# A transformer block on one core: the first layer norm, its modulation and the first projection in another order

## The chip, the core and the metric

The kernel runs on one NeuronCore of one Trainium2 chip. The core has a matrix engine (PE, TensorE), a vector engine (DVE), a scalar engine (ACT), a general engine (POOL) and a queue engine (SP) that here only issues DMA loads. Engines run side by side and wait for each other by semaphores. The metric is the device time of one execution in microseconds (us), and of several executions the median.

## The reference

The program computes two transformer blocks on 256 tokens of width 1024 in float32. Only its beginning is touched:

```python
mod = jax.nn.silu(c) @ cond_w + cond_b              # (1, 6144)
shift1, scale1, gate1, shift2, scale2, gate2 = jnp.split(mod, 6, axis=-1)
h = layer_norm(x) * (1.0 + scale1[:, None, :]) + shift1[:, None, :]
p = h @ w_in                                        # 1024 -> 2816
u = p[..., :512] * jax.nn.sigmoid(p[..., 512:1024])
# ... a causal convolution of u, a recurrence over the rest of p, an expert layer,
# and a second block with attention, a gated recurrence and a feed-forward layer
```

## The kernel before, in words

Weights stream through a ring of four slots of 2 MB. `weight_blocks` lists them in the order of their loads: a name, the slot, and the matmul job after which the slot is free. SP goes through this list in order, and where a slot was used before it waits until that job is computed, holding back every later load. `cond` blocks hold 512 columns of `cond_w`, `w_in` blocks 512 columns of `w_in`.

PSUM has eight banks. `JOBS` lists PE's work in order, each job with the engine (`act` or `dve`) that empties its bank. `assign_banks` gives banks to the jobs in rotation, and `begin` makes PE wait until the job that had the bank before was emptied. A job is a small group of matmuls: a shift of the rotation changes what a later job waits for.

The first stage goes as follows. DVE normalises the two tiles of 128 tokens into `xn`. For each of four blocks (order 2, 0, 3, 1; blocks 2 and 3 are `scale1`, 0 and 1 `shift1`) PE multiplies silu(c) with the block in four strips (`modp`, L809), DVE adds the bias into `mod_sum` (L2113), and PE adds the strips up with a matrix of ones, so that every partition holds the same 512 values (`mod`, L815). DVE multiplies and adds them onto 512 columns of `xn` (L2130, L2137). PE transposes those columns (`x_T`, L795), ACT copies them to `hT` (L1525). So the left 512 features (blocks 2 and 0) are ready before the right 512 (blocks 3 and 1).

Then comes the projection of 1024 features, eight groups of 128 (`k`). Jobs `in_conv` 2 and 3 make the gate half, 0 and 1 the other half, each 256 outputs for 256 tokens. `in_conv` 2 takes plain float32 matmuls (L782, two records each). All others are split: weight and input are each cut into a rounded high part and the rest, and three products high x high, high x low and low x high go into one sum (L840 to L842, 48 products for one job). The high parts are made by ACT (`hi_h1` L1583, `hi_in` L1590), the low ones by DVE (L2145, L2150). Between `in_conv` 2 and 3 PE transposes the parameter vectors (`params`, L872), which ACT copies to `col`. ACT takes the sigmoid of `in_conv` 2 and 3 (L1598), and its order is written out: four `hi_h1`, three `hi_in`, then the first sigmoid.

From there the work is one long chain over all engines; no part of it is touched, apart from banks that come in another rotation.

Of the kernel before, what the change touches and what calls it, by code (L numbers as in the profile page):

```python
# [77 lines left out]
IN_TWO_BANKS = ("inv_w", "inv_n")  # L78
# [94 lines left out]
BEGINS_AHEAD = {("query", 4): [("y2", 0, i) for i in range(2)], ("mem_T", 0, 0): [("y2", 1, i) for i in range(2)]}  # L173


HELD_FROM = {("in_rw", 6): (("conv_acc",), 1), ("query", 1, 0): (("h2_P", 0), 2), ("y2", 0, 0): (("h2_P", 1), 2)}
HELD_UNTIL = {("conv_mean",): (("conv_acc",), 1), ("mem_T", 0, 0): (("h2_P", 0), 2), ("mix_T", 0, 0): (("h2_P", 1), 2)}


def assign_banks():  # L180
    bank_of, before = {}, {}
    job_in, kept, turn = [None] * BANKS, set(), 0
    for job, _ in JOBS:
# [12 lines left out]
        if job in bank_of:  # L196
            kept.remove(bank_of[job])
            continue
        ahead = BEGINS_AHEAD.get(job, [])
        for j in ahead + [job]:  # L200
            n = 2 if j[0] in IN_TWO_BANKS else 1
# [6 lines left out]
            if j in ahead:  # L208
                kept.add(b)
# [51 lines left out]
def block_kernel(nc, A, out):  # L261
    ctx = ExitStack()
    with ctx:
# [13 lines left out]
        emptied = {"act": sem("emptied_by_act"), "dve": sem("emptied_by_dve"), "dots": sem("u_free"), "conv": sem("conv_ready")}  # L277
# [5 lines left out]
        turn["conv_acc",] = ("conv", 1)  # L283
        for t in range(NT):
            turn["h2_P", t] = ("dots", (t + 1) * PEER_H * TOPK)
        h2_banks = [PS[:, BANK_OF["h2_P", t]:BANK_OF["h2_P", t] + 2, :].rearrange("p a b -> p (a b)") for t in range(NT)]

        def bank(*name):
            return PS[:, BANK_OF[name], :]

# [105 lines left out]
        xn = at(12800, NT, D)  # L396
        chunk_decay = st[:, 32:48].rearrange("p (a b) -> p a b", b=NCH)
# [84 lines left out]
        def source(kind, *i):  # L482
# [5 lines left out]
            if kind == "cond":  # L488
                return lambda s: [(slot_cols(s, 512), cols(A["cond_w"], 512 * i[0], 512 * i[0] + 512))]
            if kind in ("w_in", "w_in_2"):  # L490
# [47 lines left out]
        for name, s, _ in BLOCKS:  # L538
            loads = source(*name)(s)
            landed[s] += 16 * len(loads)  # L540
# [21 lines left out]
        def loaded(eng, *name):  # L562
            s, n, _ = place[name]
            eng.wait_ge(slot_in[s], n)
# [24 lines left out]
        def _(sp):  # L589
# [3 lines left out]
            for name, s, free_after in BLOCKS:  # L593
                loads = place[name][2]
                if s in before and loads:
# [156 lines left out]
        def _(pe):  # L752
# [8 lines left out]
            def begin(*name):  # L761
# [4 lines left out]
                for job in JOB_BEFORE[name]:  # L766
                    was_emptied(pe, *job)
                return two_banks(*name) if name[0] in IN_TWO_BANKS else bank(*name)

# [2022 lines left out]
```

## Time and profile before

| | |
|---|---|
| median of three runs | 1421.1 us (1416.89, 1421.1, 1421.59) |
| the profiled execution's own time | 1416.83 us |
| its span, first to last instruction | 1414.4 us |
| mean granted TensorE clock | 0.904 of full |
| busy PE / DVE / ACT / POOL | 81% / 62% / 36% / 40% |
| chain that ended last | PE 51%, issue 12%, POOL 11%, DVE 11%, DMA 8%, ACT 3% |

Busy shares are averages over stages with other limits. The chain is read by its pieces: each has what was worked on, and the next one begins where the last one released it.

### The profile page before, as it was taken

To read this page: it belongs to the slowest core of one execution; us is meant where nothing else is said; L and a number is where in the kernel's file an instruction comes from. 1 tells how busy PE (TensorE), PEld (TensorE's weight loads), DVE (VectorE), ACT (ScalarE), POOL (GpSimd) and SP (SyncE) were. 2 spreads that over 40 slices of the span, in tenths; PEclk is the share of its full clock that TensorE was granted. 3 is DMA by queue.
4 is the path that set the end of the run, shared out by engine and by line. 5 is a ranking of instruction groups with operands and counts; after the bars stand their busy time and mean duration, and the time that the engine had idled before them with its cause. 6 is when DMAs were issued, how large, how long until landed. Compare 5 with 4: busy or idle time off the path is not lost.

```text
span 1414.4 us, 18085 instructions
## 1 busy us (share of the span) xinstructions
PE 1140.7 (81%) x6572; PEld 752.3 (53%) x6572; DVE 880.6 (62%) x1692; ACT 507.5 (36%) x1100; POOL 565.1 (40%) x641
## 2 busy tenths in 40 slices
PE   4999799848987757775879577767769998899997
PEld 1877564734553323332344233323329986799985
DVE  3588666854456458645685586567376575588763
ACT  1574332232241323222433233132216554366551
POOL 5064500325536666666756666766630000000000
PEclk9999999979999887887889888878789999899999
DMA  9372626588979999999999999999995425355440
GB/s 353 130 253 69 233 83 218 216 318 299 377 277 385 356 375 349 377 361 365 375 324 351 362 368 370 375 371 372 353 339 206 152 68 171 127 186 165 179 141 30
DMA packets 139775, 381.14 MB, mean 269 GB/s; under 512 B 10707, under 2 KB 37742, under 8 KB 139706
## 3 DMA queue, kind: packets, MB, share of 16 engines
q0 software_dynamic: 73728, 268.47, 50.3%
q1 hardware_dynamic: 64656, 108.87, 22.3%
q10 hardware_dynamic: 1322, 2.85, 0.6%
q8 instruction: 47, 0.77, 0.2%
q14 instruction: 22, 0.18, 0.0%
HBM read 379.10 MB, written 1.05 MB: 269 GB/s over the span
## 4 chain that ended last, share of the span: by engine, by line
PE 51%; issue 12%; POOL 11%; DVE 11%; DMA 8%; ACT 3%; another core or an unknown queue 1%; DVEq 1%; ACTq 0%; SPq 0%; POOLq 0%
PE banks L1222 12%; PE banks L840 7%; PE banks L842 7%; PE banks L841 7%; POOL arena L740 6%; POOL arena L733 5%; PE banks L1176 4%; DMA arena<-in_peer_u,arena 4%; DVE arena L2446 4%; DMA arena<-in_peer_v,arena 3%; PE banks L782 3%; DMA weight_ring<-in_cond_w 2%; PE banks L1157 1%; PE banks L809 1%
## 5 line engine op out<-in xcount | busy, mean ns | idle before, releaser
L1222 PE MATMUL banks<-arena 128*128 128x512 f32 x1008 | 494.4, 654 | 179.7 <-issue 120.5
L1222 PEld LDWEIGHTS banks<-arena 128*128 128x128 f32 x1008 | 210.3, 212 | 460.8 <-issue 402.1
L2446 DVE SCALAR_TENSOR_TENSOR arena<-arena,banks 128x1024 f32<-128x1024 f32 x256 | 306.9, 1220 | 202.6 <-DMA arena<-in_peer_u,arena 169.9
L740 POOL DMA_INDIRECT arena<-in_peer_v,arena x256 | 242.8, 948 | 199.7 <-PE banks L1222 104.6
L733 POOL DMA_INDIRECT arena<-in_peer_u,arena x256 | 243.9, 953 | 80.7 <-issue 73.8
L842 PE MATMUL banks<-hi_h,low_slot 128*128 128x256 f32 (+2 forms) x600 | 170.0, 283 | 0.0
L1785 ACT ACTIVATE arena<-arena 128x8 f32<-128x8 f32 x32 | 6.7, 208 | 350.9 <-issue 226.5
L842 PEld LDWEIGHTS banks<-hi_h,low_slot 128*128 128x128 f32 (+2 forms) x600 | 111.9, 187 | 0.2
L840 PE MATMUL banks<-hi_h,hi_w 128*128 128x256 f32 (+1 forms) x352 | 100.8, 286 | 1.5 <-DVE lo_h L2556 1.5
L841 PE MATMUL banks<-lo_h,hi_w 128*128 128x256 f32 (+1 forms) x352 | 99.4, 282 | 0.0
L1780 ACT ACTIVATE arena<-ident,arena 128x128 f32<-128x128 f32 x256 | 78.3, 388 | 4.9 <-issue 4.2
L1792 ACT ACTIVATE arena<-arena 128x128 f32<-128x128 f32 x252 | 77.1, 388 | 3.4 <-issue 0.5
L1176 PE MATMUL banks<-hT,weight_ring 128*128 128x128 f32 (+1 forms) x384 | 62.9, 323 | 14.9 <-issue 13.4
L698 POOL TENSOR_TENSOR arena<-arena 128x512 f32<-128x512 f32 x30 | 43.0, 1434 | 73.2 <-ACT arena L1640 71.7
L1176 PEld LDWEIGHTS banks<-hT,weight_ring 128*128 128x128 f32 x384 | 57.4, 203 | 21.2 <-issue 16.1
L840 PEld LDWEIGHTS banks<-hi_h,hi_w 128*128 128x128 f32 (+1 forms) x352 | 66.6, 189 | 1.7 <-DVE hT L2538 1.7
L841 PEld LDWEIGHTS banks<-lo_h,hi_w 128*128 128x128 f32 (+1 forms) x352 | 66.7, 189 | 0.0
L2737 DVE SCALAR_TENSOR_TENSOR arena<-banks,col,arena 128x255 f32<-128x255 f32 (+3 forms) x88 | 38.4, 477 | 30.2 <-ACT arena L2046 29.4
L2567 DVE TENSOR_TENSOR low_slot<-weight_ring,hi_w 128x2048 fp32r<-128x2048 f32 (+1 forms) x22 | 49.3, 2242 | 1.7
L721 POOL COPY arena<-arena 128x16 uint32<-128x16 uint32 x16 | 3.3, 204 | 103.0 <-DVE arena L2426 103.0
L2046 ACT ACTIVATE arena<-banks,col 128x256 f32<-128x256 f32 (+1 forms) x44 | 22.5, 562 | 56.2 <-PE banks L842 56.2
L1533 ACT ACTIVATE st<-st,eps 128x1 f32<-128x1 f32 x18 | 5.1, 293 | 102.3 <-DVE st L2098 52.0
(394 smaller groups left out, 1908.0 us busy)
## 6 DMA issues: line engine op xcount, KB each, us to landing
weight_ring<-in_cond_w SPq DMA_DIRECT2D x12, 2048.0 KB, 9.3
weight_ring<-in_w_in SPq DMA_DIRECT2D x11, 2048.0 KB, 8.0
weight_ring<-in_ffn_w_up SPq DMA_DIRECT2D x20, 1024.0 KB, 6.8
weight_ring<-in_ffn_w_down SPq DMA_DIRECT2D x5, 2048.0 KB, 7.7
weight_ring<-in_w_out SPq DMA_DIRECT2D x4, 2048.0 KB, 7.7
weight_ring<-in_peer_wq SPq DMA_DIRECT2D x4, 2048.0 KB, 8.0
arena<-in_peer_u,arena POOLq DMA_INDIRECT x256
arena<-in_peer_v,arena POOLq DMA_INDIRECT x256
```

The lines of the kernel that those rows point to most:

```text
L698: signal(g.tensor_tensor(conv[:, 2:4, :], conv[:, 2:4, :], taps(k), ALU.add), sem("taps_added"))
L733: g.indirect_dma_start(u_rows[:, j, :], None, A["peer_u"], bass.IndirectOffsetOnAxis(ap=row, axis=0)).then_inc(sem(f"u_in_{j}"), 16)
L740: g.indirect_dma_start(v_rows[:, j, :], None, A["peer_v"], bass.IndirectOffsetOnAxis(ap=row, axis=0)).then_inc(sem(f"v_in_{j}"), 16)
L840: mm(out_, sh, mh, start=first, stop=False)
L841: mm(out_, sh, ml, start=False, stop=False)
L842: return mm(out_, sl, mh, start=False, stop=last)
L1176: last = mm(b[:, half * n:half * n + n], w[:, k, f * P:f * P + P], hT[:, k, tok], start=(k == 0), stop=(k == KD - 1))
L1222: last = mm(acc[i], diag[:, r, j, :], v_rows[:, j, i * 512:(i + 1) * 512], start=False, stop=ends and j == 7)
L1780: fn(gate_diag[:, j, :], ident[:, :], ACT.Copy, scale=gates[:, bass.ds(n * TOPK + (8 * r + j), 1)])
L1792: ins = fn(diag[:, r, j, :], gate_diag[:, j, :], ACT.Copy, scale=gz[:, r, j:j + 1])
L2446: ins = v.scalar_tensor_tensor(out=u_rows[:, j, :], in0=u_rows[:, j, :], scalar=1.0, in1=h2_banks[t], op0=ALU.mult, op1=ALU.mult, accum_ou ...
L2567: signal(v.tensor_tensor(dst, w, hi_w[:, i % 4, :, 0:n], ALU.subtract), sem("up_split"))
```

## The change

Seven things are changed, all but the last in the stage up to `in_conv` 3:

1. PE transposes all of `xn` as soon as it is normalised, 16 transposes, into four banks that are held for it (`x_P`).
2. For blocks 0 to 3 the sum over strips is taken the other way round: `mod_sum` is the stationary operand and one column of ones the moving one, four matmuls of one column. The result is 4 columns with a feature on each partition. DVE copies them to `mod_col` and adds 1 to the scale.
3. ACT makes `hT` from the transposed banks with scale and shift as columns, one instruction for each of the eight groups. DVE's four multiplications and four additions over 512 columns go.
4. `w_in` block 1 (for `in_conv` 2 and 3) is loaded in two halves of 1 MB: groups 0 to 3 as third load, ahead of `cond` 3 and 1, with a semaphore of its own; groups 4 to 7 behind `cond` 1. `cond` 2 goes to slot 3, which `cond` 1 takes over, so SP waits for `modp` 2 there.
5. PE does groups 0 to 3 of `in_conv` 2 ahead of `modp` 3, and of `in_conv` 3 ahead of `mod` 3. The other halves stand where the whole jobs stood.
6. ACT and DVE make the high and low parts for both in halves too.
7. `in_conv` 2 and 3 take two banks each, and the rotation of banks changes for the jobs behind them, up to the expert layer.

```diff
-IN_TWO_BANKS = ("inv_w", "inv_n")
+IN_TWO_BANKS = ("inv_w", "inv_n", ("in_conv", 2), ("in_conv", 3))
@@ JOBS
-JOBS += part_jobs(3)
-JOBS += [(("x_T", t, 0), "act") for t in range(NT)]
-JOBS += modulation_jobs(3) + part_jobs(1) + modulation_jobs(1) + [(("x_T", t, 1), "act") for t in range(NT)]
+for _b in (3, 1):
+    JOBS += part_jobs(_b) + modulation_jobs(_b)
@@ banks
+BEGINS_AHEAD = {("modp", 3): [("in_conv", 2)], ("mod", 3): [("in_conv", 3)], ...
+HELD_FROM = {("modp", 2): (("x_P", 0), 2), ("mod", 2): (("x_P", 1), 2), ...
+HELD_UNTIL = {("modp", 3): (("x_P", 0), 2), ("in_conv", 0): (("x_P", 1), 2), ...
@@ weight_blocks
-    blocks = [(("cond", 2), 0, ("modp", 2)), (("cond", 0), 1, ("modp", 0)), (("cond", 3), 2, ("modp", 3)),
+    blocks = [(("cond", 2), 3, ("modp", 2)), (("cond", 0), 1, ("modp", 0)), (("w_in_ahead", 1), 0, None), (("cond", 3), 2, ("modp", 3)),
               (("cond", 1), 3, ("modp", 1)), (("w_in", 1), 0, ("in_conv", 3)), (("w_in", 0), 1, ("in_conv", 1)),
@@ PE
             def modulation(i):
...
+                if i < 4:
+                    for c in range(4):
+                        last = mm(b[:, c:c + 1], mod_sum[:, c * P:(c + 1) * P], ones[:, 0:1], start=True, stop=True)
+                    done(last)
...
+            def conv_tiles(half):
+                b, w = both_tiles("in_conv", 2), weights(512, "w_in", 1)
+                for e in range(2):
+                    for k in range(4 * half, 4 * half + 4):
+                        if e == 0:
+                            pe.wait_ge(sem("hT_ready"), k + 1)
+                        last = mm(b[:, e, :], w[:, k, e * P:(e + 1) * P], hT[:, k, :], start=(k == 0), stop=(k == KD - 1))
+                return last
...
+            for t in range(NT):
+                pe.wait_ge(sem("xn_ready"), t + 1)
+                for k in range(KD):
+                    last = nc.tensor.transpose(x_turned(k)[:, t * P:(t + 1) * P], xn[:, t, k * P:(k + 1) * P], ident[:, :])
+            last.then_inc(sem("x_turned"), 1)
...
+            early("in_conv", 2)
+            loaded(pe, "w_in_ahead", 1)
+            conv_tiles(0)
             mod_parts(3)
-            input_T(0)
+            early("in_conv", 3)
+            split_conv_tiles(0)
             modulation(3)
             mod_parts(1)
             modulation(1)
@@ ACT
+            def modulated(half):
+                act.wait_ge(sem("x_turned"), 1)
+                was_emptied(act, "mod", half)
+                for k in range(4 * half, 4 * half + 4):
+                    signal(fn(hT[:, k, :], x_turned(k), ACT.Identity, scale=mod_col[:, k:k + 1], bias=mod_col[:, 8 + k:9 + k]),
+                           sem("hT_ready"))
+                for k in (4 * half, 4 * half + 2):
+                    act.wait_ge(sem("hT_ready"), k + 2)
+                    signal(fn(hi_h1[:, k:k + 2, :], hT[:, k:k + 2, :], ACT.Copy), sem("h1_high"))
...
+            modulated(0)
             act.wait_ge(consts_ready, 1)
-            for p in range(3):
+            loaded(act, "w_in_ahead", 1)
+            signal(fn(hi_in[0][:, 0:4, :], in_columns(slot, *SPLIT_IN[0])[0][:, 0:4, :], ACT.Copy), sem("in_high"))
+            modulated(1)
+            in_high(0, slice(4, 8))
+            for p in range(1, 3):
                 in_high(p)
@@ DVE
+            def modulation_columns(i):
+                computed(dve, "mod", i)
+                at_ = 4 * (i % 2) + (0 if i >= 2 else 8)
+                empty(v.tensor_scalar(mod_col[:, at_:at_ + 4], bank("mod", i)[:, 0:4], 1.0, 1.0 if i >= 2 else 0.0, ALU.mult, ALU.add),
+                      "mod", i)
...
+            for half in range(2):
+                for i in (2 + half, half):
+                    mod_bias(i)
+                    modulation_columns(i)
+                low_h1(half)
+                in_low(0, slice(4 * half, 4 * half + 4))
+            for p in range(1, 3):
                 in_low(p)
```

How the rows move is shown at three places. The first is PE in the middle of the four modulation blocks, before: `slot_in_2` is the semaphore of the load of `cond` 3, `mem_kv` holds silu(c) and `mod_sum`.

```order
L809 MATMUL banks<-weight_ring,mem_kv 32x512 [waits slot_in_2]
L809 MATMUL banks<-weight_ring,mem_kv 32x512 x7
L795 MATMUL banks<-ident,arena 128x128 [waits h_ready,emptied_by_dve]
L795 MATMUL banks<-ident,arena 128x128 x7
L815 MATMUL banks<-mem_kv,ones 128x512 [waits emptied_by_dve,emptied_by_act]
L809 MATMUL banks<-weight_ring,mem_kv 32x512 [waits slot_in_3,emptied_by_dve]
L809 MATMUL banks<-weight_ring,mem_kv 32x512 x7
```

The same place now (L854 is the float32 projection, L834 `modp`, L871 to L873 the split products, of which 24 follow):

```order
L854 MATMUL banks<-hT,weight_ring 128x256 [waits ahead_in,hT_ready]
L854 MATMUL banks<-hT,weight_ring 128x256 [waits hT_ready] x3
L854 MATMUL banks<-hT,weight_ring 128x256 x4
L834 MATMUL banks<-weight_ring,mem_kv 32x512 [waits slot_in_2,emptied_by_dve]
L834 MATMUL banks<-weight_ring,mem_kv 32x512 x7
L871 MATMUL banks<-hi_h_54,hi_in_56 128x256 [waits h1_split,in_split,emptied_by_dve]
L872 MATMUL banks<-lo_h_55,hi_in_56 128x256
L873 MATMUL banks<-hi_h_54,low_slot_49 128x256
```

The transposes are gone from here, and half of `in_conv` 2 stands ahead of the strips of `cond` 3.

The second place is PE around the parameter transposes (128x54 is the first of them), before:

```order
L782 MATMUL banks<-hT,weight_ring 128x256 [waits slot_in_0,emptied_by_dve,emptied_by_act]
L782 MATMUL banks<-hT,weight_ring 128x256 x15
L872 MATMUL banks<-ident,arena 128x54 [waits emptied_by_act,params_in,consts_ready]
L872 MATMUL banks<-ident,arena 128x124
L872 MATMUL banks<-ident,arena 128x42
L872 MATMUL banks<-ident,arena 128x88 x2
L840 MATMUL banks<-hi_h_54,hi_in_56 128x256 [waits in_split,emptied_by_act,h1_split]
L841 MATMUL banks<-lo_h_55,hi_in_56 128x256
L842 MATMUL banks<-hi_h_54,low_slot_49 128x256
```

And now:

```order
L854 MATMUL banks<-hT,weight_ring 128x256 [waits slot_in_0,hT_ready]
L854 MATMUL banks<-hT,weight_ring 128x256 [waits hT_ready] x3
L854 MATMUL banks<-hT,weight_ring 128x256 x4
L926 MATMUL banks<-ident,arena 128x54 [waits emptied_by_act,params_in,consts_ready]
L926 MATMUL banks<-ident,arena 128x124
L926 MATMUL banks<-ident,arena 128x42
L926 MATMUL banks<-ident,arena 128x88 x2
L871 MATMUL banks<-hi_h_54,hi_in_56 128x256 [waits h1_split,in_split,emptied_by_dve]
L872 MATMUL banks<-lo_h_55,hi_in_56 128x256
```

Half the projection is left on either side. The bank of the parameter transposes was that of an `x_T` job before; now it is the first bank of `in_conv` 2, which ACT empties with its sigmoid.

The third place is ACT from `hT` to the first sigmoid, before. `hi_in` are the high parts of weights, `col` the parameters.

```order
L1525 ACTIVATE hT<-banks 128x4x128 [waits mm_done] x4
L1583 ACTIVATE hi_h_54<-hT 128x4x128 [waits emptied_by_act] x4
L1590 ACTIVATE hi_in_56<-weight_ring 128x2048 [waits slot_in_0,consts_ready]
L1590 ACTIVATE hi_in_57<-weight_ring 128x2048 [waits slot_in_1]
L1590 ACTIVATE hi_in_58<-weight_ring 128x2048 [waits slot_in_1]
L1598 ACT_TABLE_LOAD
L1598 ACTIVATE arena<-banks 128x2x256 [waits mm_done]
L1602 ACTIVATE col<-banks 128x396 [waits mm_done]
L1598 ACTIVATE arena<-banks 128x2x256 [waits mm_done]
```

And now:

```order
L1634 ACTIVATE hT<-banks,st 128x256 [waits emptied_by_dve,x_turned]
L1634 ACTIVATE hT<-banks,st 128x256 x3
L1638 ACTIVATE hi_h_54<-hT 128x512 [waits hT_ready] x2
L1650 ACTIVATE hi_in_56<-weight_ring 128x1024 [waits ahead_in,consts_ready]
L1634 ACTIVATE hT<-banks,st 128x256 [waits emptied_by_dve,x_turned]
L1634 ACTIVATE hT<-banks,st 128x256 x3
L1638 ACTIVATE hi_h_54<-hT 128x512 [waits hT_ready] x2
L1645 ACTIVATE hi_in_56<-weight_ring 128x1024 [waits slot_in_0]
L1645 ACTIVATE hi_in_57<-weight_ring 128x2048 [waits slot_in_1]
L1645 ACTIVATE hi_in_58<-weight_ring 128x2048 [waits slot_in_1]
L1658 ACT_TABLE_LOAD
L1658 ACTIVATE arena<-banks 128x2x256 [waits mm_done]
```

Three conversions and the table load still stand ahead of the first sigmoid; the first of them is a half, its other half being done before.

## Rows read from the trace of the kernel before

**Rows 1.** The chain that ended last, 0 to 120 us: start us, us, what.
```profile
2.83 22.32 DMA weight_ring<-in_cond_w
25.20 3.03 PE banks L809 x16
...
30.70 1.96 PE banks L809 x16
32.76 0.76 DVE mem_kv L2113
...
36.20 1.98 PE banks L795 x8
...
38.86 9.17 PE banks L782 x32
48.03 0.95 PE banks L872 x5
...
66.01 0.70 DVE arena L2164
66.78 1.92 ACT hi_in L1590
...
107.77 14.03 PE banks L782 x64
```
**Rows 2.** Timeline of PE, 0 to 49 us: start, us, operation, idle before.
```profile
11.60 3.64 PE L809 MATMUL banks<-weight_ring,mem_kv 128*32 128x512 f32 x16 [8.06 <-DMA weight_ring<-in_cond_w]
17.95 1.92 PE L809 MATMUL banks<-weight_ring,mem_kv 128*32 128x512 f32 x16 [0.62 <-DMA weight_ring<-in_cond_w]
20.83 1.12 PE L815 MATMUL banks<-mem_kv,ones 128*128 128x512 f32 x2 [0.95 <-DVE mem_kv L2113]
```
**Rows 3.** Timeline of ACT, 38 to 73 us.
```profile
38.70 2.18 ACT L1583 ACTIVATE hi_h<-hT 128x512 fp32r<-128x512 f32 x4
40.78 5.50 ACT L1590 ACTIVATE hi_in<-weight_ring 128x2048 fp32r<-128x2048 f32 x3
46.30 1.28 ACT L1598 ACT_TABLE_LOAD   x1
48.07 0.60 ACT L1598 ACTIVATE arena<-banks 128x512 f32<-128x512 f32 x1 [0.49 <-PE banks L782]
...
54.71 0.60 ACT L1598 ACTIVATE arena<-banks 128x512 f32<-128x512 f32 x1 [5.19 <-PE banks L842]
...
72.78 0.82 ACT L1609 ACTIVATE arena<-banks,keep_mu 128x256 f32<-128x256 f32 x2
```
**Rows 4.** Timeline of DVE, 34 to 50 us.
```profile
42.71 6.70 DVE L2150 TENSOR_TENSOR low_slot<-weight_ring,hi_in 128x2048 fp32r<-128x2048 f32 x3 [0.86 <-ACT hi_in L1590]
49.55 0.17 DVE L2155 TENSOR_SCALAR keep_ka<-col 128x4 f32<-128x4 f32 x1
```
**Rows 5.** Stretches of 2 us: five engines' busy us (count), PEclk, DMA share, GB/s.
```profile
26.00:28.00 2.00, 2.00 (x12) 0.21 (x4) 0.00 (x0) 0.00 (x0) 0.00 (x0) 0.50 1.06 389
...
40.00:42.00 2.00, 2.00 (x6) 1.54 (x5) 1.85 (x4) 2.00 (x3) 0.00 (x0) 0.50 1.08 360
```
**Rows 6.** Stretches of 2 us behind a pause of PE, later in the kernel.
```profile
172.00:174.00 2.00, 0.00 (x0) 0.00 (x0) 0.60 (x1) 0.00 (x0) 0.00 (x0) 1.00 0.95 354
...
176.00:178.00 2.00, 2.00 (x65) 2.00 (x63) 1.19 (x2) 0.00 (x0) 0.00 (x0) 0.51 0.03 8
178.00:180.00 2.00, 2.00 (x65) 1.88 (x61) 1.93 (x5) 1.19 (x2) 0.00 (x0) 0.63 0.00 0
```
**Rows 7.** Timeline of PE, 1208 to 1223 us: split products at either clock.
```profile
1218.05 0.41 PE L841 MATMUL banks<-lo_h,hi_w 128*128 128x256 f32 x1
...
1220.18 0.41 PE L842 MATMUL banks<-hi_h,low_slot 128*128 128x256 f32 x1
...
1220.95 0.28 PE L841 MATMUL banks<-lo_h,hi_w 128*128 128x256 f32 x1
...
1222.14 0.28 PE L842 MATMUL banks<-hi_h,low_slot 128*128 128x256 f32 x1
```

More of the change, by code:

```diff
@@ L196, in assign_banks @@
         if job in bank_of:
-            kept.remove(bank_of[job])
+            kept -= set(range(bank_of[job], bank_of[job] + banks_of(job)))
             continue
@@ L283, in block_kernel @@
         turn["conv_acc",] = ("conv", 1)
+        for i in range(2):
+            turn["x_P", i] = ("turned", 4 * i + 4)
         for t in range(NT):
@@ L539, in block_kernel @@
             loads = source(*name)(s)
+            if name[0] == "w_in_ahead":
+                place[name] = (s, 16, loads)
+                continue
             landed[s] += 16 * len(loads)
@@ L814, in modulation @@
                 was_emptied(pe, "modp", i)
-                done(mm(b, ones[:, :], mod_sum, start=True, stop=True))
-            def input_T(i):
-                was_emptied(pe, "mod", i)
-                pe.wait_ge(sem("h_ready"), i + 1)
-                for t in range(NT):
-                    b = begin("x_T", t, i)
-                    done(transposes(b, [xn[:, t, (4 * i + q) * P:(4 * i + q + 1) * P] for q in range(4)]))
+                if i < 4:
+                    for c in range(4):
+                        last = mm(b[:, c:c + 1], mod_sum[:, c * P:(c + 1) * P], ones[:, 0:1], start=True, stop=True)
+                    done(last)
+                else:
+                    done(mm(b, ones[:, :], mod_sum, start=True, stop=True))
@@ new lines, in conv_tiles, with split_conv_tiles @@
+            def conv_tiles(half):
[6 more added lines that the diff above has]
+                return last
+            def split_conv_tiles(half):
+                b = both_tiles("in_conv", 3)
+                pe.wait_ge(sem("h1_split"), 2 * half + 2)
+                pe.wait_ge(sem("in_split"), half + 1)
+                for e in range(2):
+                    f = slice(e * P, (e + 1) * P)
+                    for k in range(4 * half, 4 * half + 4):
+                        last = products(b[:, e, :], (hi_in[0][:, k, f], in_columns(low, "in_conv", 3)[0][:, k, f]),
+                                        (hi_h1[:, k, :], lo_h1[:, k, :]), k == 0, k == KD - 1)
+                return last
@@ new lines, in products @@
+            def products(out_, stationary, moving, first, last):
+                (sh, sl), (mh, ml) = stationary, moving
+                mm(out_, sh, mh, start=first, stop=False)
+                mm(out_, sh, ml, start=False, stop=False)
+                return mm(out_, sl, mh, start=False, stop=last)
+            assert not any(JOB_BEFORE["x_P", 0] + JOB_BEFORE["x_P", 1])
+            for t in range(NT):
+                pe.wait_ge(sem("xn_ready"), t + 1)
+                for k in range(KD):
+                    last = nc.tensor.transpose(x_turned(k)[:, t * P:(t + 1) * P], xn[:, t, k * P:(k + 1) * P], ident[:, :])
@@ L834, in _ @@
             modulation(1)
-            input_T(1)
-            was_emptied(pe, "x_T", 1, 1)
-            def products(out_, stationary, moving, first, last):
-                (sh, sl), (mh, ml) = stationary, moving
-                mm(out_, sh, mh, start=first, stop=False)
-                mm(out_, sh, ml, start=False, stop=False)
-                return mm(out_, sl, mh, start=False, stop=last)
             def split_in(kind, i):
@@ L1597, in _ @@
                 computed(act, "in_conv", i)
-                empty(fn(u_pad[:, 2 * (i - 2):2 * (i - 2) + 2, CONV_K - 1:], bank("in_conv", i).rearrange("p (a b) -> p a b", a=2),
-                         ACT.Sigmoid), "in_conv", i)
+                empty(fn(u_pad[:, 2 * (i - 2):2 * (i - 2) + 2, CONV_K - 1:], both_tiles("in_conv", i), ACT.Sigmoid), "in_conv", i)
                 if i == 2:
```

95 lines of the change are left out of this document (45 added, 50 removed).

## The prediction

> **What bounds the kernel now.** Read the chain that ended last first, in order of time [rows 1]. Up to 25.2 us it is the load of the modulation blocks; then come the strips of `cond` 3 and `cond` 1 on PE (L809), DVE's bias (L2113), the sum, the transposes, and at 38.86 `in_conv` 2 (L782) with 9.17 us and the parameter transposes with 0.95 us. From 49.0 to 66.0 PE works through three split jobs without a pause, and what follows is released by their ends: DVE at 66.01, ACT at 66.78. So a microsecond by which the first split job, `in_conv` 3, ends earlier is a microsecond off the whole, as long as PE then goes on. It ended at 54.6: ACT, which waited for it, starts its second sigmoid at 54.71 [rows 3]. That moment is what I forecast; the rest of the kernel is carried along.
>
> Next read ACT by its timeline [rows 3]. It is idle before 38.7 but for two copies, then it is full: four `hi_h1` (2.18), three `hi_in` (5.50), a table load (1.28), free at 47.6. There it waits 0.49 us for `in_conv` 2 and starts the first sigmoid at 48.07. Two engines arrive at nearly the same moment, and the change shortens PE's way only. Last read PE's granted clock in stretches of 2 us [rows 5]: 0.50 of full, that is 1.2 GHz, at 26 to 28 and at 40 to 42, each time behind pauses for loads or for DVE.
>
> **The first half, worked out.** `cond` 0 lands before 17.95 and its sum ends at 21.95 [rows 2]. The sum is now 8 passes with one column each, which the trace doesn't show. From above it is bounded by 8 transposes of 128 columns at the low clock, 1.98 us for L795 [rows 1], from below by half of the old sum, 0.5; I take the old 1.1. DVE's copy of 4 columns: 0.17, as L2155 [rows 4]. ACT's four `hT` of 128x256 from PSUM: 0.41 each, as L1609 (0.82 for two) [rows 3], so 1.64. PE has `hT` groups 0 to 3 at 24.0 (bounds 23.4 and 24.9). The half block of `w_in` has landed by then: it adds 1.05 MB behind `cond` 0, at some 389 GB/s [rows 5] 2.7 us, so about 20.7.
>
> `conv_tiles(0)` is 16 records. At full clock one takes 14.03/64 = 0.22 us [rows 1], so 3.5; at the low clock 2.00/6 = 0.33 [rows 5], so 5.3. It ends at 27.5 to 29.3. `cond` 3 landed at 25.2; with 1.05 MB more ahead of it that is 27.9, so it costs PE next to nothing. `modp` 3: 1.92 to 3.03 [rows 1, 2], I take the end at 31.0. Then 24 split products. At full clock one starts every 1.19/10 = 0.12 us, at the low clock every 2.13/10 = 0.21 [rows 7], so 2.8 or 5.1; I take 2.8, PE being busy since 24. With `mod` 3 PE is free at 34.9.
>
> **The second half.** `cond` 1 had landed by 30.70, when PE took it without waiting [rows 1]; 2.7 us later is 33.4 at most, unless SP, which now holds it back until `modp` 2 is done (about 15.3) [rows 2], leaves the queue empty. It doesn't: loads up to `cond` 3 are 8.4 MB, 22 us of transfers. `w_in` block 5 waits for `modp` 3, computed at 31 in place of 28.2 [rows 1]; its first reader is ACT's fourth conversion, behind `in_conv` 3. Both are hidden. So `modp` 1 runs from 34.9 to 36.8, the bias 0.76 more, the sum 1.1, the columns 0.17, with some 0.1 for each handover: ACT may start at 39.1.
>
> From here ACT is the bound. Four `hT` 1.64, two `hi_h1` of 512 2 x 0.55 = 1.1, half a `hi_in` 0.92, two whole ones 2 x 1.83 = 3.7, the table load 1.28 [rows 3]: 8.6 in all, end 47.7, and the first sigmoid, 0.60, ends at 48.3.
>
> PE meanwhile does the other half of `in_conv` 2, from 39.5 to about 43.2, and then would transpose the parameters. But their bank is now the first of `in_conv` 2, which the sigmoid must empty; the row of the order says it waits for `emptied_by_act`. Before, the same row waited for an `x_T` long emptied. So PE stands still from 43.2 to 48.3, five microseconds, with everything queued behind the transposes: the second half of `in_conv` 3 and the jobs after. They start at 48.3 where before they started at 48.03.
>
> Behind it only 24 of 48 split products are left, 2.8 in place of 5.7 us. That is what the change really brings: 54.6 − 2.8 + 0.3 = 52.1, if the clock is full. (The parameter transposes take 0.95 before and after.)
>
> **The clock.** The pause costs it. Later in this kernel PE stands still from 172 to about 175.4; at 176 to 178 the granted clock is 0.51, at 178 to 180 it is 0.63 although PE is fully busy [rows 6]. A stretch like that, some 1.7 us' worth of lost work, falls on the transposes and the 24 products, each at 0.21 instead of 0.12. The bounds are 0 (clock not taken down) and 3.3, half of the 6.5 us around 40 to 42 during which it was low, of which the middle is in the rows [rows 5]. I take 2.0, near the 1.7 and a little over, for a longer pause. So `in_conv` 3 ends at 54.1, **0.5 us earlier**.
>
> The Trainium skill, "TensorE: Matmul & The Clock Gate", section "HAM oscillation — how this bites in real kernels", says that waits between groups of matmuls take the clock to half and that the next group starts cold, and advises keeping the groups together. It speaks against cutting two jobs in halves with a wait between. By that rule the end is near 54, without it at 52.1; the trace bears the rule out at 176.
>
> **The other edits.** DVE loses 8 operations over 512 columns, two of which stood on the way to 36.20; that gain is in the sum above. Its low parts are not late: `in_conv` 0 needs the one made from 44.6 on, 2.2 us [rows 4], done by 46.9. The 16 transposes at 9 to 12 us lie before the strips of `cond` 2, taken at 11.60 [rows 2]; half a microsecond late there is hidden by the wait for `cond` 0. The new rotation of banks later on I bound by −1 and +1 and take at 0: the waits that change there are on jobs that the same matmuls read anyway, or on earlier ones.
>
> **Sum and reference.** The profiled execution took 1416.83, its span 1414.4 and 2.4 around it. It gives 1416.3. But the timed runs are 1416.89, 1421.1 and 1421.59; the kernel lands near either of two values. With the profiled one the mean of the four is 1419.1. I state the forecast from it: **1418.6 us**. A difference within 0.3%, 4.3 us, can't be told from none.
>
> **Rivals.**
> A. The pause is short or harmless. If every doubt goes the kernel's way (`cond` 1's way ends ACT's wait at 37.2, clock full) the sigmoid ends at 46.4 and `in_conv` 3 at 46.4 + 0.95 + 2.8 = 50.2: −4.4, 1414.7. For it: ACT's instructions are short and may overlap. Against: PE has 13 us of work between 24.0 and 36.8 that leaves no room for it at half clock. 0.18.
> B. The products ahead count in full, PE not waiting at the parameter transposes: 43.2 + 0.95 + 2.8 = 47.0, −7.6, 1411.5. It needs ACT to have done 8.6 us of work 5 earlier, or the transposes to be free. The order is against it. 0.07.
> C. Slower: the clock. PE is at half clock from the pause on, for the transposes, all 24 products and the first ones of `in_conv` 0, losing 3.3, and it was so in the first half too, where `conv_tiles(0)` and the products take 1.8 + 2.3 more and push ACT's start by the part that isn't covered, say 1.2. Then 54.6 − 2.8 + 0.3 + 3.3 + 1.2 = 56.6, +2.0, 1421.1. It decides from a loss of 2.5 us on. 0.20.
> D. The rotation of banks does something in the recurrence stage that I don't see, by 3 to 5 us either way. 0.07.
>
> **Chances and range.** Forecast 0.48. Its own range is 1416 to 1421, from the two values of the runs and the bounds of the clock. With A, C and most of B: 1411 to 1424. Faster by over 0.3%: B, over half of A, half of D and some of the scatter of the runs, 0.29. Slower: half of D, a little of C, scatter, 0.14. Within: 0.57.
>
> **What would show it.** Right: in the changed profile ACT's first sigmoid starts at 47 to 48.5 with no wait for PE, and PE is idle some 5 us before the transposes of 128x54, released by ACT; the granted clock behind it is near 0.5; the products before `mod` 3 are there at about 31 to 34. Rival A is seen by a sigmoid at 46 and PEclk 1.00 at 48 to 50, B by a busy PE at 44, C by more than 4 us at 0.50 behind the pause, D by equal ends of `in_conv` 3 and unequal ones at 200 us. I am wrong in my main step if PE isn't idle there, and in its size if the second sigmoid of ACT, 54.71 before, starts before 52 or after 56.

## The result, and the profile after

The changed kernel took 1432.77 us (four executions: 1429.42, 1431.53, 1434.01, 1438.82); the kernel before, in four, 1420.37. The ratio is 1.0096 [1.0057, 1.0136]: 13.6 us slower [8.1, 19.3], outside the forecast range. (Ratios here and below, with 95% intervals, are estimated from all executions and are not the quotient of the two medians, which here gives 12.4.) The profiled execution took 1431.53, its span is 1429.1, granted clock 0.898. Later, longer series (e5, e9) put the loss at ratio 1.0023, about 3 us; the interval of e9 touches 1. So there are two questions: what the first stage lost, and where the other ten microseconds were.

PE's timeline after, from the first transposes to the parameter transposes (start, us, operation, idle before and what ended it); left out are the 24 split products of `in_conv` 3 from 33.70 to 36.63 and the eight passes of `mod` 3 behind them. It answers to [rows 1, 2]:

```profile
8.86 3.67 PE L879 MATMUL banks<-ident,arena 128*128 128x128 f32 x16 [5.61 <-DVE arena L2160]
12.46 2.59 PE L834 MATMUL banks<-weight_ring,mem_kv 128*32 128x512 f32 x16
16.04 1.05 PE L842 MATMUL banks<-ones,mem_kv 128*128 128x1 f32 x8 [0.99 <-DVE mem_kv L2172]
17.96 3.25 PE L834 MATMUL banks<-weight_ring,mem_kv 128*32 128x512 f32 x16 [0.87 <-DMA weight_ring<-in_cond_w]
22.25 1.02 PE L842 MATMUL banks<-ones,mem_kv 128*128 128x1 f32 x8 [1.04 <-DVE mem_kv L2172]
25.60 6.32 PE L854 MATMUL banks<-hT,weight_ring 128*128 128x256 f32 x16 [2.33 <-ACT hT L1634]
31.85 1.92 PE L834 MATMUL banks<-weight_ring,mem_kv 128*32 128x512 f32 x16
...
37.51 1.92 PE L834 MATMUL banks<-weight_ring,mem_kv 128*32 128x512 f32 x16
40.47 1.02 PE L842 MATMUL banks<-ones,mem_kv 128*128 128x1 f32 x8 [1.03 <-DVE mem_kv L2172]
42.49 3.70 PE L854 MATMUL banks<-hT,weight_ring 128*128 128x256 f32 x16 [1.00 <-ACT hT L1634]
51.35 1.42 PE L926 MATMUL banks<-ident,arena 54*128 54x54 f32 x5 [5.15 <-ACT arena L1658]
```

The pause is there: PE has nothing to do for 5.15 us, and ACT's sigmoid (L1658) ends it. But two things are longer than in the working. The strips of `cond` 0 took 3.25 in place of 1.92, and the first half of `in_conv` 2 6.32.

ACT's timeline, which answers to [rows 3]:

```profile
23.57 1.93 ACT L1634 ACTIVATE hT<-banks,st 128x256 f32<-128x256 f32 x4 [15.63 <-DVE st L2187]
...
41.78 1.93 ACT L1634 ACTIVATE hT<-banks,st 128x256 f32<-128x256 f32 x4 [14.31 <-DVE st L2187]
43.59 1.16 ACT L1638 ACTIVATE hi_h<-hT 128x512 fp32r<-128x512 f32 x2
44.63 4.66 ACT L1645 ACTIVATE hi_in<-weight_ring 128x1024 fp32r<-128x1024 f32 x3
49.31 1.28 ACT L1658 ACT_TABLE_LOAD   x1
50.60 0.60 ACT L1658 ACTIVATE arena<-banks 128x512 f32<-128x512 f32 x1
...
57.99 0.60 ACT L1658 ACTIVATE arena<-banks 128x512 f32<-128x512 f32 x1 [4.69 <-PE banks L873]
```

From 41.78 to the first sigmoid at 50.60 ACT has 8.8 us of work without a pause. The second sigmoid starts at 57.99; before it was 54.71 [rows 3], so `in_conv` 3 ends 3.3 us later, not 0.5 earlier.

Of each stretch of 2 us the next view gives the busy us of five engines (PE first), then the granted clock, the DMA share and GB/s. These rows answer to [rows 5, 6]:

```profile
16.00:18.00 2.00, 1.09 (x12) 1.01 (x14) 0.16 (x1) 0.00 (x0) 1.66 (x6) 0.82 1.07 357
18.00:20.00 2.00, 2.00 (x12) 0.55 (x16) 0.00 (x0) 0.00 (x0) 1.19 (x5) 0.50 1.06 355
...
26.00:28.00 2.00, 2.00 (x6) 1.55 (x6) 1.78 (x3) 1.48 (x3) 0.00 (x0) 0.50 1.05 387
...
52.00:54.00 2.00, 2.00 (x11) 1.92 (x11) 0.27 (x3) 0.50 (x1) 0.00 (x0) 0.50 0.00 0
54.00:56.00 2.00, 2.00 (x11) 2.00 (x11) 0.00 (x0) 0.00 (x0) 0.00 (x0) 0.50 0.00 0
56.00:58.00 2.00, 2.00 (x12) 2.00 (x11) 0.00 (x0) 0.01 (x1) 0.00 (x0) 0.50 0.04 8
58.00:60.00 2.00, 2.00 (x18) 2.00 (x18) 0.00 (x0) 2.00 (x2) 0.00 (x0) 0.94 0.00 0
```

Behind the pause the clock stays at 1.2 GHz until about 58, over all 24 products. It had also fallen at 17 to 21 and at 24 to 31. Before, it was at 0.50 at 26 to 28 too [rows 5], but the stretches from 16 to 20 ran at full clock:

```profile
16.00:18.00 2.00, 1.17 (x6) 0.34 (x9) 0.70 (x2) 0.00 (x0) 1.59 (x6) 1.00 1.07 362
18.00:20.00 2.00, 1.88 (x16) 0.37 (x16) 0.74 (x2) 0.00 (x0) 1.19 (x5) 1.00 1.06 359
```

Where the span's 14.7 us are is read from moments found in both traces:

| moment | before | after | later by |
|---|---|---|---|
| second sigmoid starts | 54.71 | 57.99 | 3.3 |
| DVE's second `in_conv` product (L2164, now L2222) | 66.01 | 69.49 | 3.5 |
| first matmul of the recurrence stage (L1157, now L1211) | 216.34 | 219.40 | 3.1 |
| first expert matmul | 314.6 | 319.4 | 4.7 |
| last expert matmul | 1051.0 | 1065.8 | 14.8 |
| end | 1414.4 | 1429.1 | 14.7 |

The last expert matmul is read from this view of one line of the program, its instructions with their shortest, median and longest ns and the first and last start. Before, then after:

```profile
L1222 PE MATMUL banks<-arena x1008: 592/592/1222, 314.6 to 1051.0; 128*128 128x512 f32 x168
```
```profile
L1276 PE MATMUL banks<-arena x1008: 592/592/1223, 319.4 to 1065.8; 128*128 128x512 f32 x168
```

The expert stage, in which POOL gathers rows by index and nothing was changed, took 736.4 us before and 746.4 after. The first stage explains 3.3 of the difference, this stage 10. The remaining 1.4 come ahead of the first expert matmul, where traces differ by more than that: from the second sigmoid to the first expert matmul it is 259.9 us before, 261.4 after, 262.3 in e4 and 257.3 in e3, in which no instruction of that part was changed.

### The profile page after: what moved, and what is told of

It reads as the page before. It is cut to its first block, busy times and chain, and to the rows that moved or that the text cites. A ratio compares the mean times of both kernels' runs of the same rounds, so it can differ in the third digit from the quotient of the medians.

```text
span 1429.1 us, 18141 instructions
## 1 busy us (share of the span) xinstructions
PE 1146.2 (80%) x6596; PEld 760.6 (53%) x6596; DVE 878.8 (61%) x1689; ACT 508.8 (36%) x1105; POOL 565.7 (40%) x641
## 3 DMA queue, kind: packets, MB, share of 16 engines
HBM read 379.10 MB, written 1.05 MB: 266 GB/s over the span
## 4 chain that ended last, share of the span: by engine, by line
PE 50%; DVE 13%; issue 13%; POOL 11%; DMA 6%; ACT 4%; DVEq 1%; another core or an unknown queue 1%; ACTq 0%; SPq 0%; POOLq 0%
PE banks L1276 13%; PE banks L871 7%; PE banks L873 7%; PE banks L872 7%; POOL arena L763 5%; POOL arena L756 5%; DVE arena L2504 4%; PE banks L1230 4%; DMA arena<-in_peer_u,arena 3%; DMA arena<-in_peer_v,arena 2%; PE banks L807 2%; PE banks L834 1%; PE banks L1211 1%; DMA weight_ring<-in_cond_w 1%; PE banks L1341 1%
## 5 line engine op out<-in xcount | busy, mean ns | idle before, releaser
L873 PE MATMUL banks<-hi_h,low_slot 128*128 128x256 f32 (+2 forms) x600 | 171.1, 285 | 0.0
L873 PEld LDWEIGHTS banks<-hi_h,low_slot 128*128 128x128 f32 (+2 forms) x600 | 113.3, 189 | 0.2
L871 PE MATMUL banks<-hi_h,hi_w 128*128 128x256 f32 (+1 forms) x352 | 100.8, 286 | 1.5 <-DVE lo_h L2614 1.5
L871 PEld LDWEIGHTS banks<-hi_h,hi_w 128*128 128x128 f32 (+1 forms) x352 | 66.7, 189 | 1.7 <-DVE hT L2596 1.7
L2028 ACT ACTIVATE hi_w<-weight_ring 128x2048 fp32r<-128x2048 f32 (+1 forms) x22 | 41.1, 1873 | 0.7 <-DMA weight_ring<-in_ffn_w_up 0.7
```

Source lines behind the costliest of these rows:

```text
L871: mm(out_, sh, mh, start=first, stop=False)
L873: return mm(out_, sl, mh, start=False, stop=last)
```

## The experiments

Times are medians beside the kernel before on the same chip. "Second sigmoid" and "DVE" are the moments of the table's first two rows (54.71 and 66.01 before), each read from the run's one profiled execution. Of the kernel before only one trace exists.

**e1: another bank for the parameter transposes.**

```diff
             b = turn % BANKS
+            if j == ("params",):
+                b = bank_of["modp", 1]
```

> The changed kernel with one edit: the parameter transposes take the bank of modp 1, long emptied, so PE no longer waits for ACT's first sigmoid there. Theory S (the time follows the first stage one to one): the 5.15 us pause before the transposes goes, in_conv 3 ends about 7 to 9 us earlier (near 50, since PE also keeps its full clock), and the whole falls from about 1433 to 1424 to 1426; the expert stage stays about 10 us longer than in the kernel before. Theory P (the expert stage's length depends on the moment at which it starts): the first stage gains as above, but the whole may land anywhere from 1412 to 1430, with the expert stage at another length than 746 us. Theory L (the expert stage depends on where its code lies): expert stage still near 746 us, as the code is the same but for one bank number.

1415.32 against 1418.84, ratio 0.9982 [0.9952, 1.0011]. The pause is gone (PE, then ACT):

```profile
41.70 5.38 PE L856 MATMUL banks<-hT,weight_ring 128*128 128x256 f32 x16 [1.00 <-ACT hT L1636]
47.02 1.00 PE L928 MATMUL banks<-ident,arena 54*128 54x54 f32 x5
```
```profile
49.82 0.60 ACT L1660 ACTIVATE arena<-banks 128x512 f32<-128x512 f32 x1
50.31 0.50 ACT L1663 ACTIVATE col<-banks 128x396 f32<-128x396 f32 x1
50.93 0.60 ACT L1660 ACTIVATE arena<-banks 128x512 f32<-128x512 f32 x1
```

The second sigmoid starts at 50.93, 7.1 us before that of the changed kernel, and now waits only for ACT. DVE is at 62.24, 3.8 ahead of the kernel before. The bank's wait, with the low clock behind it, is the loss of the first stage. The 3.8 us are one trace against one: e4 below, the kernel before but for a few empty instructions, has DVE at 64.84, and there the gain would be 2.6. The expert stage took 740.3 us in this trace, not the 746 that two of the three theories expected.

**e2, e3, e4: does a late or otherwise shifted start lengthen the expert stage?** Three edits of the kernel before: four (e2) or two (e3) products of zeros ahead of `in_conv` 3, or a few empty instructions at the start of PE, ACT and DVE (e4).

```diff
+                if (kind, i) == ("in_conv", 3):
+                    for _ in range(4):    # e3: 2
+                        mm(b[:, :], zeros[:, :], hT[:, 0:2, :].rearrange("p a b -> p (a b)"), start=True, stop=True)
```

> The kernel before with four float32 matmuls of 128x512 on zeros put into PE's row ahead of in_conv 3's products (their result is overwritten): a delay of about 3.4 us and no other change. Theory S: +3.4 us in all, about 1423.5. Theory P: the expert stage starts 3.4 us later, as in the changed kernel (3.1 to 4.7 later there), and takes another length, so up to +12 in all, 1430 to 1433. Theory L: the few instructions more move the code by little; between +3 and +12.

> The same with two such matmuls, a delay of 1.7 us. Theory S: +1.7, about 1421.8. Theory P: another length of the expert stage again, not on a line through the kernel before and the run with four matmuls. Theory L: as the run with four.

> The kernel before with 6, 5 and 5 empty instructions at the start of PE's, ACT's and DVE's rows, executed while they wait for the first loads, so that all code behind lies a little further on and nothing starts later. Theories S and P: no change, 1420. Theory L (where the code of the expert loops lies sets their pace): a visible change, by several us, in the expert stage.

| | median | ratio | second sigmoid | profiled execution's span | its expert stage |
|---|---|---|---|---|---|
| e2 | 1423.41 | 1.0033 [1.0006, 1.0060] | 58.33 | 1428.1 | 746.4 |
| e3 | 1427.03 | 1.0072 [1.0047, 1.0098] | 53.63 | 1411.6 | 737.0 |
| e4 | 1422.18 | 1.0033 [1.0007, 1.0060] | 53.53 | 1415.8 | 736.3 |

No order by delay: the smaller one has the higher median, and e4, which delays nothing, reads +3.3 us, with an interval that leaves out 1. In e3's trace the two products did not even delay the second sigmoid. They are there with 1.92 us, but the granted clock stayed at 1.00 from 32 us on, and `in_conv` 2 in front of them took 7.17 in place of 9.17:

```profile
38.08 7.17 PE L782 MATMUL banks<-hT,weight_ring 128*128 128x256 f32 x32 [0.74 <-ACT hT L1528]
```

In e4 it took 8.75. So the untouched first stage moves by over 1 us with the clock of its execution (54.71 and 53.53), and without the two products e3's would have ended near 51.7 by the same trace, an estimate. The executions of one program tell why the medians have no order. In this series 25 of the kernel before lie between 1414.07 and 1433.68, five of e3 between 1413.84 and 1432.67. The profiled execution of e3 was its fastest, with an expert stage of 737; that of e2 was its slowest and took 746 there, as the changed kernel's. The tails don't scatter like that: behind the last expert matmul come 363.4 us before and 363.3 after. So one execution can be 10 us longer than another in the expert stage alone. That a later start lengthens it every time is spoken against by e11 (below), not by these three: there the stage starts at 318.3, as late as in e2 (317.9), and takes 739.3. What sets the medians of e3 and e4 stays open; that a mere shift of the code is worth 3 us was not excluded.

**e5: the changed kernel again**, on another chip, on which the kernel before takes 1332.2.

> The changed kernel once more, unedited, with more executions. By its trace and by the two delay runs, whose executions spread over 13 and 19 us, the 12 us have two parts: 3.4 us of the first stage, the same in every execution, and a length of the expert stage that differs from one execution to the next of the same program. Theory C (the rest was chance of four executions): median 1421 to 1426, ratio 1.001 to 1.005, the first stage the same to 0.5 us (ACT's second sigmoid at 57.5 to 58.5), the expert stage of another length than 746 us. Theory K (the changed kernel really lengthens the expert stage): median 1430 to 1435 again.

1336.45, ratio **1.0023** [1.0005, 1.0042], +3.1 us, from 12 executions against 35. Its PE row at the transposes (the pause was 2.24 here, because the half of `in_conv` 2 ahead of it ran at low clock, 6.62):

```profile
41.54 6.62 PE L854 MATMUL banks<-hT,weight_ring 128*128 128x256 f32 x16 [1.00 <-ACT hT L1634]
50.40 1.21 PE L926 MATMUL banks<-ident,arena 54*128 54x54 f32 x5 [2.24 <-ACT arena L1658]
```

The second sigmoid is at 55.78, 1.1 us late in this execution against 3.3 in the first trace: the two differ in when the clock was low. That also misses the expectation, which had the first stage the same to 0.5 us. The loss of the whole, 0.7 to 5.6 us by its interval, holds both, and not the 13.6 us of the first four executions. The whole alone doesn't prove the 3 us, since e4 reads as much with nothing delayed; the loss rests on the stage, and there it is 1.1 to 4.6 us at DVE (67.09 to 69.49 against 64.84 to 66.01).

**e6: the changed kernel with its pause filled.** Five products whose results are overwritten stand in front of the parameter transposes.

```diff
+                    was_emptied(pe, "modp", 1)
+                    for _ in range(WARM_HERE):    # 5
+                        mm(bank("modp", 1), zeros[:, :], hT[:, 0:2, :].rearrange("p a b -> p (a b)"), start=True, stop=True)
                     b = begin("params")
```

> The changed kernel with five float32 matmuls of 128x512 on zeros into an emptied bank, put into PE's pause before the parameter transposes (some 4.4 us of it). If the low clock behind the pause costs what I read from the trace (transposes 1.42 in place of 1.0, 24 products in 4.9 in place of 2.8 us), ACT's second sigmoid comes 2.0 to 2.6 us earlier, at 55.4 to 56.0 in place of 57.99, while the first stays near 50.6. If the clock isn't to blame it stays at 58, or moves later by what the extra matmuls overrun. The whole: 2 us less than the changed kernel, which the spread of the expert stage may hide.

1338.87, ratio 1.0046 [1.0024, 1.0069]. The clock behind the pause was full:

```profile
50.00:52.00 2.00, 1.56 (x11) 1.33 (x12) 1.21 (x1) 0.89 (x2) 0.00 (x0) 1.00 0.00 0
52.00:54.00 2.00, 2.00 (x19) 2.00 (x18) 0.25 (x2) 0.00 (x0) 0.00 (x0) 1.00 0.03 8
```

The first sigmoid came at 49.79, the second at 54.35: 4.6 us apart, against 7.4 in the changed kernel's first trace and 6.1 in e5. So of the loss behind the pause 1.6 to 2.8 us are the clock; the wait is the rest. The whole time did not follow: the median is 2.4 above e5, with intervals that overlap, and the traced execution was the fastest of the ten (1328.73). Why the others are longer is open.

**e7, e8: how much are the products ahead worth?** Both from e1. In e7 the 24 split products of `in_conv` 3 stand behind `mod` 1 in place of ahead of `mod` 3; in e8 the first half of `in_conv` 2 too.

```diff
             mod_parts(3)
-            early("in_conv", 3)
-            split_conv_tiles(0)
             modulation(3)
             mod_parts(1)
             modulation(1)
+            early("in_conv", 3)
+            split_conv_tiles(0)
```

> e1 (parameter transposes in another bank) with the first half of in_conv 3 moved behind mod 1, so that modp 1 doesn't stand behind its 2.9 us. In e1 PE has no pause from 41.7 on, and ACT's hT starts at 40.99. If PE's row holds the modulation up, hT starts 1.5 to 3 us earlier, but the products still have to be done: in_conv 1's end (DVE at 62.24 in e1) moves by -1 to +0.5. If the load of cond 1 is late instead, hT starts less than 1 us earlier.

> e1 with both first halves moved behind mod 1: nothing of the projection ahead of the modulation any more; transposes at once, columns on ACT and the loads in halves stay. If the products ahead are worth their time, in_conv 1 ends later than e1's 62.24 by the 2 to 5 us that PE now waits for cond 3 and cond 1 with nothing to do; it may even end no earlier than before (66.0). If PE's idle time is short, it ends within 1 us of e1.

e7: 1330.78 against 1332.2, ratio 0.9994 [0.9975, 1.0013], sigmoids at 49.84 and 50.95, as in e1. e8: 1333.77, 1.0010 [0.9990, 1.0029], sigmoids at 53.94 and 57.74, DVE 6.8 us later than in e1. So in these traces the work ahead is worth 6.8 us to the stage, with the clock's part in it. That the half of `in_conv` 3 is worth nothing is less sure: in e7 the half of `in_conv` 2 was at low clock for its whole length and ended 1.8 us later than in e1 (`modp` 3 starts at 32.83 against 31.06), which hides what leaving out 2.9 us of products may have gained. With nothing ahead ACT's second `hT` starts at 41.35, no earlier than with both (40.99), but for another reason. In e8 PE waits 6.10 us for `cond` 3 and then runs every step up to 46 us at low clock:

```profile
28.12 3.64 PE L836 MATMUL banks<-weight_ring,mem_kv 128*32 128x512 f32 x16 [6.10 <-DMA weight_ring<-in_cond_w]
32.79 1.84 PE L844 MATMUL banks<-ones,mem_kv 128*128 128x1 f32 x8 [1.02 <-DVE mem_kv L2174]
34.55 3.64 PE L836 MATMUL banks<-weight_ring,mem_kv 128*32 128x512 f32 x16
```

**e9, e10: the changed kernel and e1 side by side**, 12 executions each, on the first series' chip.

> The changed kernel, unedited, a second time, beside e10 and e11 on one chip. Theory: its steady loss is the 3.3 us of the first stage, less where the low clock is shorter, and the rest of the first 12 us was scatter of four executions. Ratio 1.001 to 1.004. Rival, the 10 us in the expert stage belong to the program: 1.006 or more.

> e1 again: the parameter transposes take the bank of modp 1 in place of the first of in_conv 2. On the same chip as e9 the two differ by the pause alone. By the stage it should be 6.8 to 7.3 us faster than e9 (second sigmoid near 50.9), and 3.8 us faster than the kernel before: ratio 0.997 to 0.999. If the programs' times aren't the sum of their stages, it is anywhere from 0.995 to 1.003.

e9: 1421.26 against 1417.12, ratio 1.0023 [0.9997, 1.0049]; e10: 1414.54, 0.9999 [0.9975, 1.0024]. Between their medians lie 6.7 us, between those of e5 and e7 5.7; the stage says 7.2 and 4.8 (DVE at 69.43 and 62.27, at 67.09 and 62.25); between the means it is 5.7 and 4.7. Drawing executions anew from those on record gives 2 to 9 and 3 to 7 us for these two, so the bank shows in the whole time (e7 differs from e5 by the moved products too). The gain over the kernel before doesn't: it was forecast as 0.997 to 0.999 and reads 0.9999, and if the first stage before can be as early as in e3 and e4, less than 3.8 us was to be had.

The executions of e9 run from 1414.58 to 1431.55, and the one profiled was the slowest, and its trace is the first one again:

```profile
L1276 PE MATMUL banks<-arena x1008: 592/592/1222, 318.7 to 1066.0; 128*128 128x512 f32 x168
```

747.3 us of expert stage at 1431.55. The first stage is that of the first trace (pause 5.15, second sigmoid at 57.94). The other eleven executions are up to 17 us shorter; the traces of the changed kernel differ by 2.2 us at the second sigmoid (55.78 in e5), so most of the 17 must be made behind it. That the expert stage makes them is inferred from the traces of other kernels above (736 to 747 us), since the short executions of e9 have no trace. Where in it the time goes can be read: from 500 to 600 us behind its start the DMA engines moved 354 GB/s in the first trace and 353 in e2 and e9, the three with 746 to 747 us, against 363 to 373 in the other traces of kernels near 1420 us. Why is open.

**e11, e12: can the early low clock be kept away?** From e1, with products of the identity in PE's waits.

```diff
+            def keep_warm(out_, n):
+                for _ in range(n):
+                    mm(out_, ident[:, :], ident[:, :], start=True, stop=True)
@@ mod_parts, i == 0
+                    keep_warm(b[:, 0:P], 3)
@@ modulation, i in (2, 0)
+                    keep_warm(b[:, 0:P], 4)
@@ ahead of conv_tiles(0)
+            keep_warm(bank("modp", 0)[:, 0:P], 8)
             early("in_conv", 2)
```

The last eight write into the bank of `modp` 0 in e12, as shown, and in e11 into the first bank of `in_conv` 2, behind `early`.

> e10 with products of the identity in PE's waits between 12 and 25 us: 4 in front of each of the first two sums, 3 in front of cond 0's load wait, 8 in front of the first half of in_conv 2, 0.22 us each; their results are overwritten. If the low clock at 18 to 20 and 24 to 30 us comes from these waits, modp 0 takes 1.9 in place of 3.3 and conv_tiles(0) 3.5 in place of 6.3; hT's second half starts 1 to 2 us earlier (39 to 40), the sigmoids with it: ratio 0.001 below e10. Rival: the load of cond 3, in the queue behind 1 MB more, bounds this place anyhow (landed near 28.1 in e8), then the clock is better and hT starts less than 0.7 earlier.

> e11 with one difference: the 8 products of the identity in front of the first half of in_conv 2 write into the bank of modp 0, which is free there. In e11 they wrote into a bank of the transposed rows, waited until hT was made of it and so stood behind the pause, for 3.75 us. Theory: now they fill the pause of about 2.3 us, conv_tiles(0) starts 0.3 to 1 us behind hT's start near 22.2, at 24 to 24.5, and takes 3.5 to 3.7 at full clock; modp 3 waits a little for cond 3 (28.1) and hT's second half starts at 38 to 39.5, against 40.99 in e1 and e10. Sigmoids near 48 and 49, against 49.86 and 50.97: 1.5 to 2.5 us better, ratio 0.996 to 0.998. Rival: cond 3 and cond 1 in the load queue bind and hT doesn't start before 40.3; or the clock falls all the same in the wait for cond 0 and conv_tiles(0) takes over 5 us.

e11: 1418.81, ratio 1.0013 [0.9984, 1.0042]. The last eight products went wrong: their bank held transposed rows, so they waited 2.37 us for `hT` and then took 3.75 themselves. `modp` 0 was at 1.92, but so it was in e5 without any filler. ACT's second `hT` started at 42.40, 1.4 us later than in e10. This trace is the one with a late start and a short expert stage:

```profile
L1287 PE MATMUL banks<-arena x1008: 592/592/1222, 318.3 to 1057.6; 128*128 128x512 f32 x168
```

e12: 1420.27 against 1423.62 on a third chip, ratio 0.9988 [0.9960, 1.0015]. PE:

```profile
17.93 1.92 PE L842 MATMUL banks<-weight_ring,mem_kv 128*32 128x512 f32 x16
...
24.17 3.69 PE L864 MATMUL banks<-hT,weight_ring 128*128 128x256 f32 x16 [0.44 <-ACT hT L1645]
28.09 1.92 PE L842 MATMUL banks<-weight_ring,mem_kv 128*32 128x512 f32 x16 [0.23 <-DMA weight_ring<-in_cond_w]
...
38.74 6.67 PE L864 MATMUL banks<-hT,weight_ring 128*128 128x256 f32 x16 [1.00 <-ACT hT L1645]
```

With the clock full the first half takes 3.69, where the seven traces with this half ahead and no filler before it have 5.41 to 6.74, and ACT's second `hT` starts at 38.03, which was forecast as 39.1. The sigmoids come at 46.85 and 49.26; the second now waits 1.41 for PE, since the clock fell in the short waits around 38 and the second half took 6.67. DVE is at 60.56, 5.4 ahead of the kernel before and 8.9 ahead of the changed one, both traced on another chip or in another series than this one. By that it is the best first stage of all; the whole time shows no difference from before that stands clear of the scatter, and neither does that of e1, e7 or e10.

## Why the prediction was wrong

**What held.** The mechanism: the parameter transposes wait for the sigmoid, PE idle 5.15 us (forecast: some five; 2.24 in e5), ACT the bound with 8.8 us of work (8.6), the clock at 0.50 behind it. The rotation of banks cost nothing up to the recurrence stage (3.3 late at 55 us, 3.1 at 216); behind it nothing can be told from the scatter. Moving loads was hidden. Without the pause, rival B's −7.6, the stage gained 3.8 (e1).

**Step "PE has `hT` groups 0 to 3 at 24.0 ... I take the end at 31.0".** It was the mis-sized term. `modp` 0 was not looked at: it was taken over with its 1.92 [rows 2], but ran at low clock, 3.25; `conv_tiles(0)` began at 25.6 and took 6.32, above the bound of 5.3: that was made by dividing 2 us by the six records of a stretch [rows 5], which is too coarse; at low clock one takes 0.42 (6.67 for 16 in e12). `modp` 3 ended at 33.7, 2.7 late, and ACT's `hT` at 41.78 was 2.7 late as well. The working took the middle between the two clocks for these steps, and full clock for the products because PE would be busy from 24; the products did run at full clock (2.9), but the clock had already fallen when `conv_tiles(0)` began, and it stayed low nearly to its end. In e12, where it had not fallen, `modp` 3 ended at 30.0 and `hT` began at 38.03. How much this term costs differs from one execution to the next: in e5, the same program, `modp` 0 took 1.92, the tiles still 6.74, and `hT` began at 40.84, 1.7 late:

```profile
17.92 1.92 PE L834 MATMUL banks<-weight_ring,mem_kv 128*32 128x512 f32 x16 [1.11 <-DMA weight_ring<-in_cond_w]
```

**Step "some 1.7 us' worth of lost work ... I take 2.0".** Transposes and products took 6.6 us from 51.35 to 57.9 against 3.75 at full clock: 2.8. The stated bound of 3.3 held. Together 2.7 + 0.8, and 0.3 of longer ACT work and handover, are the 3.8 between the forecast end of 54.1 and the measured 57.9. That is rival C's mechanism in both its parts: its sign, more than 4 us at 0.50 behind the pause, is there with over 6. But it had 1.2 for the first half, where 2.7 were lost, and it expected the products ahead at low clock, which they were not. The size was outside the stated bounds for the stage (a second sigmoid after 56) in the first trace and e9, and inside in e5, at 55.78.

The rule from the Trainium skill, "TensorE: Matmul & The Clock Gate", section "HAM oscillation — how this bites in real kernels", which the prediction set beside its row, held behind the pause, where the clock was at 0.50, and cost 2.8 us where the row had suggested 1.7.

**The scatter: step "the kernel lands near either of two values".** The range was made from runs between 1416.9 and 1421.6, as if the kernel had two values. It has a spread: 25 executions between 1414 and 1434, 29 between 1412 and 1426. A median of four can be 10 us off, and this one was: e9 has 1421.26 for the same program, where the kernel before takes 1417.12. In the profiled one of the four it was the expert stage; the other three have no trace. A forecast with the right stage (+3.3) would have said 1422 to 1423 and also missed 1432.8.

## What to carry to other kernels

When a job gets a second bank, look at who inherits its banks: a small job in between that had a free bank before may now wait for the slowest reader, with everything queued behind it. Ask of every stretch with waits at which clock it will run, also where PE isn't idle for long, and price all products behind it at that clock, to the end of the chain of steps. And don't take the clock of one trace for that of the program: two traces of the same kernel had it low in different places. And know the spread of one program before reading a difference of 1% out of a few executions; read the stage that was changed first, and ask of a difference anywhere else whether a second trace of the same program has it too.

## What the runs showed of the hardware that was not expected

- The clock can fall without a long pause, and not in every execution. Ahead of it PE had done 16 transposes, the strips and eight one-column passes, with waits of 0.99 and 0.87 us; at 18 to 20 us it was at 0.50 in the first trace and in e9, and at 1.00 in e5, the same program with waits of 0.98 and 1.11. Products of the identity in the waits aren't shown to matter there. At 24 to 28 us they may: the clock was at 1.00 from 14 to 36 us in e12, and no trace without them had it full over `conv_tiles(0)`. Whether the transposes or the one-column sums brought it down was not tried apart.
- The granted clock in the view's first rows is not borne out by the durations. It reads 1.00 at 8 to 14 us, but the first strips took 3.64 us in the kernel before, as at 0.50 in e8, and 1.92 at full clock; the 16 transposes took 3.67, where eight take 1.10 at full clock (e3) and 1.97 at low. In e2 it reads 1.00 even at 16 to 18, where the two passes of 512 columns took 2.08 in place of 1.12. By the durations the clock was low there; for the stretches from 16 to 20 shown above view and durations agree.
- Transposes alone were enough for the clock to rise: in e7 PE did nothing but these 16 from 8.85 us on, behind 5.25 us without work, and the weight loads of the first took 0.231 us, those of the last 0.141.
- A sum with one moving column saves next to nothing: its 8 passes take 1.02 to 1.05 us at full clock, the two passes of 512 columns took 1.12 [rows 2]; at low clock the 8 take 1.83 (e8).
- One execution of a program differs from the next by up to 20 us of 1420, by the traces that there are mostly in the stage with the indexed gathers. And one of the chips ran the whole kernel in 1332 us in place of 1420: from the first gather to the last expert matmul it took 703.1 us in e5 and 797.3 in e9, the same program, with 398 and 349 GB/s moved over the expert stage.
